# Attention values of a hybrid decoder step issued one unit later, in one block with the next step's turning and the following step's scores

## What is computed

```
proj = rmsnorm(x) @ w_in                 # -> q, k, v, B, C, u, gate_a, gate_b
a    = window_attention(rope(q), rope(k), v, sinks)   # blocks of 128 queries, window 128, 16 heads, 2 kv heads
b    = B * causal_dwconv3(C * u)
x   += rmsnorm((sigmoid(ga) * (a @ w_attn_branch) + sigmoid(gb) * (b @ w_conv_branch)) @ w_o)
x   += rmsnorm((gelu(causal_dwconv3(up)) * gt) @ w_ffn_down)
x   += sigmoid(x @ w_ple_gate) * (p @ w_ple)
```

## Time and profile before

| what | value |
|---|---|
| time, 3 runs | 2648.56, 2649.84 (median), 2652.91 us |
| the profiled execution's own time | 2651.19 us |
| its span | 2649.4 us |
| PE busy | 2635.8 us, 99% |
| PEld busy | 2575.1 us, 97% |
| DVE busy | 2265.1 us, 85% |
| ACT busy | 1415.0 us, 53% |
| POOL busy | 195.2 us, 7% |
| mean granted clock of TensorE | 0.999 |

### The profile page before, as it was taken

One profiled execution on the slowest core, in us unless ns is written; L12 is line 12 of the kernel. 1 busy time (PEld: TensorE's weight loads), 2 busy tenths in 40 slices (PEclk: granted clock), 3 DMA queues, 4 the chain that ended last, 5 costly groups with the idle time before them and its releaser, 6 DMA issues.

```text
span 2649.4 us, 55478 instructions
## 1 busy us (share of the span) xinstructions
PE 2635.8 (99%) x20853; PEld 2575.1 (97%) x20853; DVE 2265.1 (85%) x4000; ACT 1415.0 (53%) x2592; POOL 195.2 (7%) x296
## 2 busy tenths in 40 slices
PE   9999999999999999999999999999999999999999
PEld 8999999999999999999999999999999999999899
DVE  7988888888889987898888888888888768789987
ACT  6544545555565555655555555555555454445454
POOL 0221000000011000000000000000000000000000
PEclk9999999999999999999999999999999999999999
DMA  6676434433486555655566655665569575565774
GB/s 229 185 206 184 135 116 138 140 129 113 165 276 211 165 165 160 243 177 162 167 207 187 177 166 167 190 196 177 159 187 307 159 237 175 161 207 163 249 264 151
DMA packets 162481, 487.12 MB, mean 184 GB/s; under 512 B 17337, under 2 KB 51521, under 8 KB 158928
## 3 DMA queue, kind: packets, MB, share of 16 engines
q1 hardware_dynamic: 129184, 372.41, 40.0%
q0 software_dynamic: 32976, 112.38, 19.1%
q10 hardware_dynamic: 144, 0.15, 0.0%
HBM read 426.42 MB, written 57.30 MB: 183 GB/s over the span
## 4 chain that ended last, share of the span: by engine, by line
PE 65%; DVE 2%; DMA 1%; issue 1%; ACT 0%; DVEq 0%; ACTq 0%
PE pair L1199 55%; PE pair L1164 4%; PE pair L1298 2%; PE pair L1102 2%; PE pair L1276 1%; DMA s_one<-in_sstream 1%; DVE v_lo L1959 0%; DVE lo L2333 0%; ACT o_hi L1433 0%; PE pair L1059 0%; ACT v_hi L1368 0%; DVE lo_A L2333 0%; DVE raw L2293 0%; DVE s_raw L2277 0%; DVE s_raw L2258 0%
## 5 line engine op out<-in xcount | busy, mean ns | idle before, releaser
L1199 PE MATMUL pair<-o_hi,v_hi 128*128 128x260 f32 x5840 | 1656.0, 284 | 1.2 <-DVE v_lo L1959 0.8
L1199 PE MATMUL pair<-o_hi,v_lo 128*128 128x260 f32 x5840 | 1648.9, 282 | 0.0
L1368 ACT ACTIVATE v_hi<-s_raw 128x512 fp32r<-128x512 f32 (+1 forms) x1384 | 862.9, 627 | 882.6 <-PE pair L1199 786.2
L1199 PE MATMUL pair<-lo,v_hi 128*128 128x260 f32 x4172 | 1178.6, 283 | 0.0
L1959 DVE TENSOR_TENSOR v_lo<-s_raw,v_hi 128x512 fp32r<-128x512 f32 (+1 forms) x1288 | 874.8, 682 | 297.4 <-ACT v_hi L1368 260.4
L1199 PEld LDWEIGHTS pair<-o_hi,v_hi 128*128 128x128 f32 x5840 | 1098.0, 188 | 14.8 <-issue 11.9
L1199 PEld LDWEIGHTS pair<-o_hi,v_lo 128*128 128x128 f32 x5840 | 1099.9, 188 | 0.0
L1199 PEld LDWEIGHTS pair<-lo,v_hi 128*128 128x128 f32 x4172 | 784.1, 188 | 0.2
L1368 ACT ACTIVATE v_hi<-s_one 128x512 fp32r<-128x512 f32 (+1 forms) x228 | 142.5, 628 | 201.4 <-PE pair L1199 164.1
L1199 PE MATMUL pair<-lo_E,v_hi 128*128 128x260 f32 x834 | 236.0, 283 | 0.0
L1199 PE MATMUL pair<-lo_A,v_hi 128*128 128x260 f32 x834 | 235.1, 282 | 0.0
(11 more groups left out here) (301 smaller groups left out, 2609.5 us busy)
## 6 DMA issues: line engine op xcount, KB each, us to landing
s_raw<-in_sstream SPq DMA_DIRECT2D x468, 512.0 KB, 5.0
s_one<-in_sstream POOLq DMA_DIRECT2D x168, 512.0 KB, 5.2
raw<-f_scr SPq DMA_DIRECT2D x12, 1040.0 KB, 7.6
s_raw<-in_sstream SPq DMA_DIRECT2D x32, 384.0 KB, 3.9
g_scr<-d_h SPq DMA_DIRECT2D x16, 520.0 KB, 2.8
g_in<-g_scr SPq DMA_DIRECT2D x32, 260.0 KB, 8.3
x_scr<-y_sb SPq DMA_DIRECT2D x8, 1040.0 KB, 5.1
s_one<-in_sstream POOLq DMA_DIRECT2D x32, 256.0 KB, 5.5
```

Source lines behind the costliest of these rows:

```text
L1199: mm = pe.matmul(out, wt[:, slot, kk * P:kk * P + P], r[:, k, :], start=j in (0, 1, 3) and k == 0 and n == 0, stop=k == nk - 1 and n == 2, ...
L1368: nc.scalar.activation(v_hi[:, n % 4, 0:width], src, ACT.Copy, scale=0.5 if halved(u) else 1.0).then_inc(v_hi_rdy, 1)
```

## The change

`values(n)` moves on PE from the middle of unit u + 1 to the place ahead of unit u + 2, in front of `turn(n + 1)` and `scores(n + 2)`, by a new table `VALUES`. What hangs on it moves along: `attention_out` to i = 9 of unit u + 2, and the four forms of a complete group to i = 11 to 13 of unit u + 2 (units 21, 25 and 29 instead of 20, 24 and 28). `VALUES` holds units 15, 18 and 20 to 31. In unit 31 `values(14)` goes after product 4, in front of `turn(15)`; the copy of step 13 is made at i = 2 there. The program of POOL is not changed.

```diff
 TURN = {u + 1: n for u, n in ATT.items() if u != LAST}
+VALUES = {u + 1: n for u, n in TURN.items() if u != LAST}
...
                 here = {}
-                if u in TURN or u in ATT:
-                    here[-1] = lambda: (turn(TURN[u]) if u in TURN else None,
+                if u in VALUES or u in TURN or u in ATT:
+                    here[-1] = lambda: (values(VALUES[u]) if u in VALUES else None,
+                                        turn(TURN[u]) if u in TURN else None,
                                         scores(ATT[u]) if u in ATT else None)
-                if u in TURN:
-                    here[3] = lambda: values(TURN[u])
                 if u == LAST:
-                    here[4] = lambda: turn(ATT[u])
+                    here[4] = lambda: (values(TURN[u]), turn(ATT[u]))
                     here[5] = lambda: values(ATT[u])
...
-                if u in TURN and i == 9:
+                if u in VALUES and i == (2 if u == LAST else 9):
+                    attention_out(VALUES[u])
+                if u == LAST and i == 9:
                     attention_out(TURN[u])
...
-                if u in TURN and TURN[u] % 4 == 3 and i in (11, 12, 13):
-                    attention_form(TURN[u] // 4, {11: 1, 12: 2, 13: 4}[i])
+                if u in VALUES and VALUES[u] % 4 == 3 and i in (11, 12, 13):
+                    attention_form(VALUES[u] // 4, {11: 1, 12: 2, 13: 4}[i])
                     if i == 13:
-                        attention_form(TURN[u] // 4, 6)
+                        attention_form(VALUES[u] // 4, 6)
```

## The result

The changed kernel takes 2679.91 us (2679.11 to 2682.80), against 2649.89 us (2648.56 to 2652.91) of the kernel before: ratio 1.0115, 95% interval 1.0103 to 1.0128. Slower, as forecast, by 30.0 us where 28.0 were forecast. The profiled execution took 2679.4 us with a span of 2677.6.

A forecast was written before the change was run, and what follows sets the result against it. PE bounds the kernel, busy 2635.8 of 2649.4 us. Waits 23.7 plus low clock 4.3 less joining 0 give +28.0 us on the median 2649.8: 2677.8 us, 1.06% slower, range 2664 to 2688.

The forecast's parts named there:

- Three waits of PE: Ahead of scores in units 22, 26, 30: query load late behind POOL's wait for forms, 23.7 us in all (20.1 to 28.5).
- Forecast 7.9 us: Each PE wait for the query load: landing at 494.3 less scores' possible start at 486.43; bounds 6.7 and 9.5 us.
- The argument for 4.0 instead of the 5.6 of the earlier trace: Query load's landing: gate store can't go out while PE waits, so only two stores are ahead; 4.0 us from issue.
- DVE was not late in units 14 and 17: Middle of units: PE reaches i = 8 up to 1.21 us sooner, 0.27 us of cover left in unit 17; costed at nothing.
- Joining saves nothing: 14 values visits joined to another visit on PE: saving taken as 0, bounded above by 14 x 0.33 = 4.6 us.
- the 0.11 us: Price of one matmul in a values visit on PE: four matmuls more cost 0.44 us.
- The clock: Granted clock falls to 0.50 behind each of three PE waits: 3 x 1.4 = 4.3 us, bounds 0 and 8.6.
- The rival with twice the length (8.6): Clock stays low longer behind each long wait: 23.7 + 8.6, total 2682.1 us; chance 0.1.
- The estimate from the figure of the Trainium skill: Clock falls behind the three waits, priced from another kernel's figure: 2.5 us in all, total 1.8 us lower.
- a shift there: Branch stage: its fall of the clock may shift with the rest; allowed for in the range 2664 to 2688 only.

The follow-up runs named there:

- e1: Changed kernel, but POOL stores each group's forms one loop turn later, behind the next query load (n = 4, 8, 12): 2647.34 us, ratio 0.9994.
- e3: Changed kernel; POOL still waits for the forms at n = 3, 7, 11, then issues the query load ahead of the two stores: 2669.79 us, ratio 1.0078.
- e4: Kernel before, plus a POOL wait for DVE's results of units 21, 25, 29 behind the stores of groups 0 to 2: 2670.91 us, ratio 1.0080.
- e6: Kernel before with only POOL's order changed, stores behind the next query load: 2649.94 us against 2649.45, ratio 1.0001.
- e2: Changed kernel with 17 extra matmuls on PE ahead of the query-load wait in the scores of steps 6, 10 and 14: 2690.99 us.
- e5: Changed kernel with 9 extra matmuls on PE ahead of the query-load wait in the scores of steps 6, 10 and 14: 2673.75 us, ratio 1.0090.
- e7: As e1, but the stores of group 2 stay ahead of the query load of step 14 (n = 11): 2658.68 us, ratio 1.0032.

## Why the prediction was right

- *Where and how often.* Three waits of PE ahead of the scores in units 22, 26 and 30, ended by the load of q_blk. They are there, nowhere else, and e1 takes all of them away by POOL's order alone.
- *How long.* Forecast 7.9 us, measured 8.1. Its terms: issue of the load 5.34 us behind PE's last product (490.35 - 485.01), measured 5.39; landing 4.0 forecast, 4.1 measured. The argument for 4.0 instead of the 5.6 of the earlier trace rows, that the gate store can't go out while PE waits, held: it went out at 523.39. The load landed after 5.6 us with the two stores ahead and the gate store of SP behind it, after 4.1 with the stores alone, and after 2.6 with nothing ahead of it (e3). The Trainium skill ("DMA: Bandwidth & Descriptors", Issuing engines are not separate DMA queues) says that transfers of all issuing engines run on the same 16 DMA engines and interleave; these landings agree with it. No run takes the gate store away by itself.
- *Nothing moved costs by itself.* DVE was not late in units 14 and 17; no wait of PE for it appears there. e1 and e4 show the two halves: all moved work and no late load, no loss; a late load and no moved work, a loss.
- *Joining saves nothing.* Taken as 0 by the one joint visit of before, bounded at 4.6 us. Measured 0.04 us a time, 0.6 in all, and the stretch of e1 is 0.6 us shorter than that of before. One reading ahead of the prediction is wrong without harm to the sum: `scores` and `values` issue four matmuls, not eight (`values` two where blk is 0), and each fp32 matmul has two records. So the 0.11 us is the price of a record, and the counts of the rows are records.
- *The clock.* The mechanism was right, the term too small: 3 x 1.4 = 4.3 us forecast, 8.0 measured. I took the length of the fall from the earlier trace rows, behind a wait of 1.95 us. Behind 8.1 us the clock was down already when PE began again, and came back after 5.4 to 6.2 us. The rival with twice the length (8.6) was the nearer one. The estimate from the figure of the Trainium skill ("TensorE: Matmul & The Clock Gate", HAM oscillation), 2.5 us in all, was further off.
- *Why the total came out near all the same.* The ledger has 31.6 us in the stretch of the change, 3.6 more than forecast, nearly all of it the clock's term. By the medians the whole is 30.0: some of the 31.6 came back outside the stretch, in the profiled execution mostly at the first seam of the branch stage, with a shorter wait and no fall behind it. The prediction named a shift there as a term of the range, not of the sum, so that it made the total come out nearer is luck. That the change has a part in it isn't shown: the wait at that seam differs among the runs from 0.8 to 1.95 us, and it is 0.8, with no fall, in e6, which moves nothing on PE.

## What to carry to other kernels

When work is moved to a later point, look at what waits for its result, and then at what stands behind that wait in the same queue: here a store had to wait one unit longer, and a load that had nothing to do with it stood behind. A queue written as one loop couples things by their order alone; put the load that an engine will need next ahead of the wait for something that nobody needs soon. And price a stall of TensorE with what comes behind it: each of these cost 1.8 to 2.8 us more than the waiting itself.

## What the runs showed of the hardware

- Behind a wait of PE of 4.8, 5.0 or 8.1 us the granted clock was 0.50 when it began again, and the low clock cost 2.5 to 2.6 us (e4, 4.8), 1.8 to 2.3 (e3, 5.0) and 2.4 to 2.8 (the changed kernel, 8.1), so it hardly went by the length of the wait. Extra matmuls during the wait kept it at 1.00 (e2, e5).
- Behind shorter waits the fall is not certain. In the branch stage waits of 0.8 to 1.8 us had none behind them in any trace. Of the waits of 1.85 to 1.95 us, six had one (both of before, and the second seam of after, e1, e3 and e4) and three had none (e2 1.91, e6 1.85, e7 1.90). The length of such a wait alone doesn't tell which it will be.
- An fp32 matmul with 512 columns took two records of 0.43 us on PE (e2: 34 records in 14.76 us for 17 matmuls), and the four matmuls of `scores` have eight records, while transposes came as one record each (64 for 16 turns of four). Counting records against the matmuls in the code of the kernel before would have shown it ahead of e2.
- Turn, scores and values cost PE on joining what they cost apart, within 0.04 us: what a visit pays beyond its columns isn't paid for leaving the main stream. That it is paid for each change of shape is a guess; no run here separates it.
